# Means of the heads' squared outputs taken from two rounded parts, and taken four half-products later

## The reference

```python
x = x + 0.5 * swiglu(rmsnorm(x, n1), f1g, f1u, f1d)
h = rmsnorm(x, nmix)
q, fpre, vin, gout, xr, yr, ga, gb = split(h @ w_in)          # eight blocks of 1024 columns
f = lb + (1 - lb) * sigmoid(fpre)
oA = hgrn2_chunked(silu(q), log(f), 1 - f, vin)               # 8 heads of 128 x 128 state
oA = oA * rsqrt(mean(oA * oA, axis=-1) + EPS)                 # per head: the part that is changed
oA = oA * o_norm * silu(gout)
oB = rglru(conv(xr)) * gelu(yr)
m  = sigmoid(ga) * (oA @ w_a_up) + sigmoid(gb) * (oB @ w_b_up)
x  = x + m @ w_out
x  = x + 0.5 * swiglu(rmsnorm(x, n3), f2g, f2u, f2d)
```

## Time and profile before

| | |
|---|---|
| median of 3 runs | 2466.42 us (2466.25 to 2466.57) |
| the profiled execution, its own time | 2467.49 us |
| its span, first to last instruction | 2465.6 us |
| TensorE busy | 2437.9 us (99%) |
| VectorE busy | 1739.1 us (71%) |
| ScalarE busy | 1272.5 us (52%) |
| GpSimd busy | 177.3 us (7%) |
| mean granted TensorE clock | 0.997 |

### The profile page before, as it was taken

The page is one execution under the profiler, slowest core; times in us unless marked ns, Lnnn a source line. Parts: engine busy times, 40 slices in busy tenths (PEclk is TensorE's granted clock), DMA queues, the critical chain, the costliest instruction groups (busy, mean ns, idle before and its releaser), DMA issues.

```text
span 2465.6 us, 51450 instructions
## 1 busy us (share of the span) xinstructions
PE 2437.9 (99%) x19240; PEld 2410.5 (98%) x19241; DVE 1739.1 (71%) x2916; ACT 1272.5 (52%) x2125; POOL 177.3 (7%) x210
## 2 busy tenths in 40 slices
PE   9999999999999999999999999999999999999998
PEld 8999999999988999999999999999999999999997
DVE  7767777777688888887777766543576667776777
ACT  5355555555456656555666665211434555555553
POOL 0011111111130000000000000000200111111110
PEclk9999999999999999999999999999999999999999
DMA  3355555555631334333322225432123555555555
GB/s 126 121 121 120 120 120 123 123 122 120 162 142 43 89 94 110 80 86 95 115 77 94 77 94 210 143 119 89 35 70 103 122 125 122 123 124 124 123 124 187
DMA packets 137254, 278.40 MB, mean 113 GB/s; under 512 B 67009, under 2 KB 71489, under 8 KB 136641
## 3 DMA queue, kind: packets, MB, share of 16 engines
q1 hardware_dynamic: 114112, 192.46, 23.7%
q0 software_dynamic: 23040, 84.55, 18.1%
HBM read 154.86 MB, written 114.77 MB: 109 GB/s over the span
## 4 chain that ended last, share of the span: by engine, by line
PE 93%; DVE 3%; DMA 1%; ACT 1%; issue 1%; SPq 0%; DVEq 0%; ACTq 0%
PE banks L154 30%; PE banks L155 29%; PE banks L156 29%; PE banks L1828 1%; PE banks L1805 1%; PE banks L1770 1%; DVE mix_blk_lo L508 1%; PE banks L1791 0%; PE banks L1799 0%; DMA x_sum<-f_snap 0%; PE banks L1801 0%; DVE mix_blk_f L484 0%; ACT mix_blk_hi L500 0%; PE banks L444 0%; DMA x_sum<-f_part 0%
## 5 line engine op out<-in xcount | busy, mean ns | idle before, releaser
L154 PE MATMUL banks<-f_blk_hi,f_u_hi 128*128 128x258 f32 x2496 | 707.1, 283 | 0.3
L155 PE MATMUL banks<-f_blk_lo,f_u_hi 128*128 128x258 f32 x2496 | 705.6, 283 | 0.0
L156 PE MATMUL banks<-f_blk_hi,f_u_lo 128*128 128x258 f32 x2496 | 704.8, 282 | 0.0
L154 PE MATMUL banks<-mix_blk_hi,mix_u_hi 128*128 128x258 f32 x1808 | 519.0, 287 | 2.5 <-DVE mix_blk_lo L508 1.8
L155 PE MATMUL banks<-mix_blk_lo,mix_u_hi 128*128 128x258 f32 x1808 | 511.6, 283 | 0.0
L156 PE MATMUL banks<-mix_blk_hi,mix_u_lo 128*128 128x258 f32 x1808 | 510.8, 283 | 0.0
L154 PEld LDWEIGHTS banks<-f_blk_hi,f_u_hi 128*128 128x128 f32 x2496 | 471.4, 189 | 2.0 <-issue 0.8
L156 PEld LDWEIGHTS banks<-f_blk_hi,f_u_lo 128*128 128x128 f32 x2496 | 471.2, 189 | 0.0
L155 PEld LDWEIGHTS banks<-f_blk_lo,f_u_hi 128*128 128x128 f32 x2496 | 470.8, 189 | 0.2
L154 PEld LDWEIGHTS banks<-mix_blk_hi,mix_u_hi 128*128 128x128 f32 x1808 | 342.9, 190 | 5.0 <-DVE mix_blk_lo L508 2.4
L155 PEld LDWEIGHTS banks<-mix_blk_lo,mix_u_hi 128*128 128x128 f32 x1808 | 342.4, 189 | 0.9
(11 more groups left out here) (290 smaller groups left out, 4361.5 us busy)
## 6 DMA issues: line engine op xcount, KB each, us to landing
raw<-w_slabs SPq DMA_DIRECT2D x220, 512.0 KB, 3.4
x_sum<-f_part POOLq DMA_DIRECT2D x126, 516.0 KB, 7.7
x_sum<-f_snap POOLq DMA_DIRECT2D x18, 516.0 KB, 10.3
x_sum<-x POOLq DMA_DIRECT2D x16, 516.0 KB, 6.2
x<-x_sum SPq DMA_DIRECT2D x16, 516.0 KB, 8.5
sg_kept<-sgt SPq DMA_DIRECT2D x8, 1032.0 KB, 5.6
sgs<-sg_kept SPq DMA_DIRECT2D x16, 516.0 KB, 4.5
x<-x_t SPq DMA_DIRECT2D x8, 516.0 KB, 8.0
```

The source lines that it names most:

```text
L154: pe.matmul(out, wh, xh, start=start, stop=False, skip_group_check=chained)
L155: pe.matmul(out, wh, xl, start=False, stop=False, skip_group_check=chained)
L156: return pe.matmul(out, wl, xh, start=False, stop=stop, skip_group_check=chained)
```

## The change

- `finish_high` (new, ScalarE): a rounded copy `sq_hi` of the squares. `finish_low` (new, VectorE): the remainder `sq_lo`, written over `sq`. Both have 1032 columns.
- `core_means`: each of the three float32 matmuls becomes two `fp32r` matmuls that add up in PSUM, on `sq_hi` and on `sq_lo`. The matrix of 1/128 is a rounded copy `ones_r`, made once by VectorE in `plain_vector`.
- `core_means` is called behind half 6 instead of half 2.
- ScalarE, groups 1 to 7: the first snap goes ahead of the square, `finish_high` behind it; both early highs and the second snap go ahead of `finish_log`.
- VectorE, groups 1 to 7: instead of four sums and then the first mix, there are one sum, the first mix, two sums, `finish_low`, the fourth sum. The second mix goes ahead of `turn_keys`. `keys` has one more wait, for the means, because `sq_hi` lies where `ke` lies.
- Group 8: `finish_high` behind the first snap, the second snap ahead of `finish_log`; on VectorE the first mix and `finish_low` go ahead of the sums.

```diff
     for n in range(2):
         dve.memset(s.sc[n][:, :], 0.0).then_inc(s.zeroed, 1)
+    dve.wait_ge(s.zeroed, 1)
+    dve.tensor_copy(k.ones_r[:, :], k.ones_h[:, :]).then_inc(s.zeroed, 1)
...
     dve.wait_ge(s.key, keyed(j))
+    wait(dve, s.mean_ready, j * 3)
     dve.tensor_copy(s.ke[:, SEQ:T], s.f[:, SEQ:T])
...
 def core_means(pe, k, s, h):
 
-    pe.wait_ge(s.squared, h * 1 + 1)
+    pe.wait_ge(s.squared, h * 3 + 3)
     pe.wait_ge(s.vm_ready, h * 4 + 4)
     for t in range(NT):
-        pe.matmul(k.bank[MEAN_BANKS[t]][:, 0:TG], k.ones_h[:, :], s.sq[:, tg(t)], start=True, stop=True)\
+        out = k.bank[MEAN_BANKS[t]][:, 0:TG]
+        pe.matmul(out, k.ones_r[:, :], s.sq_hi[:, tg(t)], start=True, stop=False)
+        pe.matmul(out, k.ones_r[:, :], s.sq_lo[:, tg(t)], start=False, stop=True)\
             .then_inc(s.mean_ready, 1)
...
+def finish_high(act, k, s, h):
+    act.wait_ge(s.squared, h * 3 + 1)
+    act.activation(s.sq_hi[:, :], s.sq[:, :], ACT.Copy).then_inc(s.squared, 1)
+
+
+def finish_low(dve, k, s, h):
+    dve.wait_ge(s.squared, h * 3 + 2)
+    dve.tensor_tensor(s.sq_lo[:, :], s.sq[:, :], s.sq_hi[:, :].bitcast(F32), ALU.subtract).then_inc(s.squared, 1)
...
         def beside_finish(half):
-            if half == 2 and kind != LRU:
+            if half == 6 and kind != LRU:
                 core_means(pe, k, s, j - 1)
...
     def head_pair(j):
         h = j - 1
         pair_high(act, k, s, j, 1, 6)
+        snap(act, k, s, j, 1, 0)
         finish_square(act, k, s, h)
+        finish_high(act, k, s, h)
         log_decay(act, k, s, j)
-        snap(act, k, s, j, 1, 0)
-        ahead(j + 1, 0, (0,))
+        ahead(j + 1, 0, (0, 1))
+        snap(act, k, s, j, 1, 1)
         finish_log(act, k, s, h)
-        ahead(j + 1, 0, (1,))
-        snap(act, k, s, j, 1, 1)
         exp_decay(act, k, s, j)
         snap(act, k, s, j, 1, 2)
         finish_rstd(act, k, s, h)
...
         snap(act, k, s, j, 1, 0)
+        if kind == LAST_HGRN:
+            finish_high(act, k, s, j - 1)
         ahead(j + 1, 0, (0, 1), edge)
         if kind == LAST_HGRN:
+            snap(act, k, s, j, 1, 1)
             finish_log(act, k, s, j - 1)
             finish_rstd(act, k, s, j - 1)
         else:
             lru_root(act, k, s, j - 9)
-        snap(act, k, s, j, 1, 1)
+            snap(act, k, s, j, 1, 1)
...
         h = j - 1
         affine(dve, k, s, j)
         pair_low(dve, k, s, j, 1, 6)
-        sums(j + 1, 0, range(4))
+        sums(j + 1, 0, (0,))
         wait(dve, s.values_turned, j * 2 - 2)
         mix(dve, k, s, j, 1, 0, s.vb[:, half(0)])
+        sums(j + 1, 0, (1, 2))
+        finish_low(dve, k, s, h)
+        sums(j + 1, 0, (3,))
         cumulate(dve, k, s, j)
         turn_values(dve, k, s, j, 0)
         ahead(j + 1, 0, (0,))
         keys(dve, k, s, j)
         ahead(j + 1, 0, (1,))
+        mix(dve, k, s, j, 1, 1, s.snap_t[2][:, :])
         turn_keys(dve, k, s, j)
-        mix(dve, k, s, j, 1, 1, s.snap_t[2][:, :])
         finish_vector(dve, k, s, h, first)
...
+        if kind == LAST_HGRN:
+            mix(dve, k, s, j, 1, 0, s.snap_t[0][:, :])
+            finish_low(dve, k, s, j - 1)
         sums(j + 1, 0, range(4), edge)
...
+    k.ones_r = Region(fixed.at - 4 * P, fixed.at).put("ones_rounded", [P, P], F32R)
...
+    k.mid.sq_hi = Region(r.at, end).put("sq_hi", [P, T], F32R)
     k.mid.ke = r.put("ke", [P, T], F32)
     k.mid.qe = r.put("qe", [P, T], F32)
     k.mid.vm = Region(r.at, end).put("vm", [P, DEC, P], F32R)
+    k.mid.sq_lo = Region(r.at, end).put("sq_lo", [P, T], F32R)
     k.mid.sq = r.put("sq", [P, T], F32)
```

More of the change, by code:

```diff
@@ L2231, in core_pair @@
         if first:
-            act.wait_ge(s.zeroed, 5)
+            act.wait_ge(s.zeroed, 6)
         for hf in range(1, 14):
@@ L2360, in core_pair @@
                 dve.memset(tile[:, :].bitcast(F32), 0.0).then_inc(s.zeroed, 1)
-            dve.wait_ge(s.zeroed, 5)
+            dve.wait_ge(s.zeroed, 6)
         else:
@@ L2439, in recurrent_pair @@
             lru_mult2(dve, k, s, j - 9)
-        mix(dve, k, s, j, 1, 0, s.snap_t[0][:, :])
+            mix(dve, k, s, j, 1, 0, s.snap_t[0][:, :])
         ahead(j + 1, 0, (0, 1), edge)
@@ L2443, in recurrent_pair @@
             finish_vector(dve, k, s, j - 1)
-            dve.wait_ge(s.zeroed, 6)
+            dve.wait_ge(s.zeroed, 7)
         else:
```

## The result

| | before | after |
|---|---|---|
| median | 2466.21 us (8 runs, 2464.97 to 2466.72) | 2472.72 us (8 runs, 2470.62 to 2475.59) |
| ratio | | 1.0028, 95% interval 1.0019 to 1.0038 |
| span of the profiled execution | 2465.6 us | 2471.1 us |
| TensorE, VectorE, ScalarE busy | 2437.9, 1739.1, 1272.5 us | 2434.2, 1748.7, 1281.5 us |

What follows compares the result with a forecast made beforehand. TensorE is 99% busy, but VectorE's full chain ending round c = 1 releases it. Groups 2 to 7 +6.5, group 1 +0.8, group 8 -1.4, copy +0.2: +6.1 on 2466.42 gives 2472.5 us, range 2465.5 to 2477.

Steps and rivals of the forecast that it cites:

- The means' price: TensorE, each head: six fp32r matmuls take 0.94 us in place of 1.74, 0.80 us less.
- VectorE's chain in groups 2 to 7: Round c = 1: first mix 1.74 us earlier, 2.96 us added behind it to the old 13.78 us.
- The step per group: Groups 2 to 7, end of round c = 1: next round begins 1.09 us later, 6.5 us in all.
- the release: End of round c = 1: 0.14 us from the third mix's end to TensorE's start.
- The snap as a second floor: TensorE waits about 0.7 us ahead of product 5, adding nothing; the round could be no shorter than 21.9 us.
- Group 1: Round c = 1: third mix ends at 820.72, TensorE goes on at 820.86 instead of 820.04, +0.8 us.
- Group 8: Means save 0.80 us, second snap's wait saves 0.83, third snap's new wait costs 0.25: -1.4 us.
- The copy: Rounded copy of the matrix, made once on VectorE: 0 to 0.4 us, taken as 0.2.
- The range: ±0.25 us on seven groups' steps, 0.2 on the copy, 0.4 on group 8: 2469.5 to 2475.5 us.
- TensorE's saving comes through: Rival, end of round c = 1, groups 1 to 7: every head saves 0.80 us, 2459.6 us; chance 0.14.
- The lag runs on into the recurrence: Rival, round c = 0: 0.3 to 0.6 us more per group, 2476 us; chance 0.06.
- The clock falls: Rival: TensorE's clock halves behind the new waits, 12 us more, 2484 us; chance 0.05.

Runs made afterwards that it cites:

- e8: e7 with the means as three float32 matmuls again, without the split: 2469.59 us, ratio 1.0012.
- e7: e6 with VectorE's first copy of scores ahead of remainders 4, 5 and 6: 2465.81 us, ratio 0.9997.
- e0: The changed kernel once more, with no further edit: 2473.07 us, ratio 1.0027.
- e2: The changed kernel with ScalarE's third snap ahead of the second and third Exp: 2473.65 us, ratio 1.0031.
- e1: The changed kernel with the second and third sum back ahead of the first mix on VectorE: 2467.58 us, ratio 1.0004.
- e10d: e9d with the third snap ahead of the third high part in group 8: 2463.87 us, ratio 0.9991.
- e6: e3 with the third mix ahead of finish_vector, ScalarE's highs and take ahead of its gates, one remainder of c = 0 later: 2465.98 us, ratio 0.9998.
- e3: The changed kernel with the edits of e1 and e2 together: 2468.15 us, ratio 1.0005.
- e9d: e7 with one remainder moved behind turn_keys and the keys' DMAs ahead of a weight row on SyncE: 2463.67 us, ratio 0.9992.
- e5: The changed kernel with one more 1032-column VectorE operation ahead of the remainder in groups 1 to 7: 2480.57 us, ratio 1.0058.
- e6_again: e6 repeated unchanged, beside e7 and e8: 2465.58 us, ratio 0.9997.

## Why the prediction was right

The time was forecast at 2472.5 and is 2472.7. Point by point:

- **The means' price.** 0.94 us forecast, 0.95 measured; e8 against e7 shows 0.76 per round c = 1 for the split alone (0.80 forecast).
- **VectorE's chain in groups 2 to 7.** The first mix was forecast at 6.11 us into the round (856.94 - 850.83) and came at 6.12 (856.83 - 850.71). The remainder is 1.23 us long and the next operation starts 1.14 behind its start, as taken from the earlier trace rows. From the first mix to the third mix's end: 16.71 us (873.54 - 856.83), forecast 13.78 + 2.96 = 16.74. (By the Trainium skill, "VectorE: DVE Perf Modes", The DRAIN you can't avoid, the next operation does not start until the pipeline is empty, which would have made it the full 1.23; this trace does not bear that out. The prediction left out what the same section adds: a next operation that is not held back starts earlier. A start 0.09 us ahead of the previous end fits that.)
- **The step per group.** +1.09 forecast, +1.00 measured (5.99 / 6). The term that was off is the release: 0.14 us from the mix's end to TensorE's start was taken from a release by ScalarE in group 8; by VectorE it is 0.05 (873.59 - 873.54). What was left out is 0.11 us of lost pace behind the wait, which falls into round c = 0: 7 x 0.11 = 0.77, and the measured growth there is 0.86 (0.76 in e0). Over seven groups the first is some 0.6 us too much and the second some 0.8 too little; that they cancel is luck.
- **The snap as a second floor.** 0.7 us forecast ahead of product 5, 0.72 measured. That it adds nothing is shown by e2, and that the round then stays at about the old length by e1 (22.05; the forecast said no shorter than 21.9), where the Exp is a third floor beside it.
- **Group 1.** +0.8 forecast, +0.72 measured.
- **Group 8.** The wait for the second snap went as forecast. The new one for the third snap is 0.20 us by the bracket (0.25 forecast), and e10d takes it away for 0.10 of a round. The round is 21.55 (21.4 forecast). A new wait of 0.25 us for `lw_lo` in group 9 accounts for the +0.24 behind it.
- **The copy.** 0.2 forecast. VectorE spends 0.08 us on it from start to start (736.17 to 736.25). In the trace the stretch ahead of group 1 is shorter by 1.03 for another reason, so no price can be read for it.
- **The range.** Its three terms, 1.75, 0.2 and 0.4, add up to 2.35 us, and the range stated is 3 us either way. The measured time lies 0.2 from the middle, inside both.

Of the rivals, *TensorE's saving comes through* was refuted by the waits; e6 and e7 show what it would take. *The lag runs on into the recurrence* did not happen beyond the 0.11 us. *The clock falls* did not happen at any of the new waits. Where the gain went is therefore shown, not argued. It is waited away behind VectorE's chain of the last 16.7 us of the round, into which 1.8 us of sums and 1.14 us of remainder were put. Two of the three sums account for most of the loss (e1: 5 us of 6.5). With them back the round is still 0.15 us longer than before (e3: 22.05 against 21.90), because VectorE then waits for the Exp behind the later means; so nothing of the 0.80 comes through.

What stays open: the best order tried, e9d, is 1.8 us below before, and its interval reaches to 1.0001, so by itself it isn't shown to be faster. With e10d, which differs in one snap, there are 22 runs of median 2463.8, and 14 of them lie below the lowest of the 21 runs of before beside them (2464.10); that points to a small gain, of some 1.7 us. Its rounds c = 1 are 0.78 us shorter than before, its rounds c = 0 0.2 to 0.9 longer, and 1.8 in group 2. Whether an order exists in which the recurrence takes the earlier start without waiting was not found. A kernel with the means back at half 2 and split was not tried, although e3 points at the later means as the next thing to take back: VectorE would have to write the remainder ahead of the first mix, in the time that it now spends waiting.

## What to carry to other kernels

An engine that is 99% busy can gain nothing from cheaper work if an engine that releases it has a full chain. Before moving work across a wait, read the idle entry ahead of the waiting instruction: work ahead of it lies in idle time, the same work behind it is added to the chain in full (here 1.13 us a round for the 1.14 us operation of e5). When one wait is taken away, look for what is ready next: here the mix, the Exp, the snap, the keys' DMA and the copy of `qe` followed one another within 1 us each, and the reorderings together were worth under 2 us against before.

## What the runs showed of the hardware

**An idle stretch and the clock.** In the profiled execution of before, the granted clock falls near 715 us, in code that the change does not touch; in that of after it does not. Windows of before, then of after (length; busy us of each engine; clock; DMA share; GB/s):

```profile
711.00:714.00 3.00, 2.48 (x21) 2.27 (x20) 3.00 (x4) 1.04 (x3) 2.52 (x4) 1.00 0.82 352
714.00:717.00 3.00, 2.04 (x10) 1.80 (x10) 1.86 (x3) 1.30 (x3) 0.54 (x1) 0.76 1.46 528
717.00:720.00 3.00, 3.00 (x13) 2.14 (x12) 0.00 (x0) 0.74 (x2) 0.00 (x0) 0.67 0.52 212
```

```profile
711.00:714.00 3.00, 2.57 (x22) 2.36 (x20) 3.00 (x4) 1.32 (x4) 2.52 (x4) 1.00 0.82 352
714.00:717.00 3.00, 1.95 (x10) 1.50 (x11) 2.12 (x4) 1.31 (x3) 0.81 (x1) 1.00 1.47 528
717.00:720.00 3.00, 3.00 (x22) 2.63 (x21) 0.70 (x2) 1.66 (x5) 0.00 (x0) 1.00 0.42 158
```

Ahead of it TensorE was idle twice in a row in both, by almost the same amounts. In before:

```profile
713.81 0.39 PE L154 MATMUL banks<-mix_blk_hi,mix_u_hi 128*128 128x258 f32 x1 [0.52 <-DVE mix_blk_lo L508]
715.40 0.48 PE L154 MATMUL banks<-mix_blk_hi,mix_u_hi 128*128 128x258 f32 x1 [0.95 <-DVE mix_blk_lo L508]
```

In after:

```profile
714.08 0.38 PE L154 MATMUL banks<-mix_blk_hi,mix_u_hi 128*128 128x258 f32 x1 [0.51 <-DVE mix_blk_lo L508]
715.66 0.39 PE L154 MATMUL banks<-mix_blk_hi,mix_u_hi 128*128 128x258 f32 x1 [0.96 <-DVE mix_blk_lo L508]
```

Of the fourteen profiles seven show this fall (clocks of 0.76 and 0.67 over 3 us each lose 0.72 + 0.99 = 1.7 us, which is 3.4 us at 1.2 GHz) and seven don't. The fall behind the 2.07 us of the earlier trace rows is in thirteen. In e6_again the windows behind a wait of 2.08 us, which ended at 765.30, show 1.00 up to 772, and the clock is below full only in the window from 772 to 776 (0.88), in which another idle stretch, of 1.99 us, ends at 774.41. So the same code with the same idle times can meet the fall in one execution and not in another. None of the new waits brought one, not even e2's six of 1.57 to 1.66 us (the clock in the windows behind each of them is 1.00). The prediction placed the danger between 0.98 and 2.07 us for a single stretch; nothing up to 1.66 brought a fall here. (The Trainium skill, "TensorE: Matmul & The Clock Gate", What's actually happening, lets the gate follow recent activity. That two short stretches close together were followed by a fall in half of the profiles, and single ones of up to 1.66 us in none, does not contradict it; what decides between the halves no run here shows.)

**A wait costs more than its bracket.** The brackets of the two waits in group 2 say 0.56 and 0.81 us. By the starts of the matmuls they cost 0.72 + 0.08 and 0.97 + 0.11. Seven or eight times each that is some 13 us, where the waits view adds up to 9.6.
